# Seven half-size products for eight pairs of projected tiles

## The reference, cut to what matters

```python
h = rmsnorm(x, P['norm1_w'][l]) * (1 + sc1) + sh1
u_att, u_rw, u_ssd = split_cols(h @ P['w_in'][l], [ATT_COLS, RW_COLS, SSD_COLS])
```

## Time and profile before

| what | value |
|---|---|
| median of 3 runs | 1047.29 us (1043.87 to 1050.62) |
| the profiled execution | 1050.17 us |
| its span, first to last instruction | 1048.4 us |
| mean granted TensorE clock | 0.966 of full speed |
| TensorE busy | 929.7 us (89% of the span) |
| VectorE busy | 492.1 us (47%) |
| ScalarE busy | 286.3 us (27%) |

### The profile page before, as it was taken

One profiled execution on the slowest core, in us unless ns is written; L12 is line 12 of the kernel. 1 busy time (PEld: TensorE's weight loads), 2 busy tenths in 40 slices (PEclk: granted clock), 3 DMA queues, 4 the chain that ended last, 5 costly groups with the idle time before them and its releaser, 6 DMA issues. The chain is left out here.

```text
span 1048.4 us, 25535 instructions
## 1 busy us (share of the span) xinstructions
PE 929.7 (89%) x11081; PEld 663.2 (63%) x11081; DVE 492.1 (47%) x1349; ACT 286.3 (27%) x664; POOL 61.9 (6%) x91
## 2 busy tenths in 40 slices
PE   7899998777789999979989999887789999996796
PEld 4455566566668876646755566666677977664455
DVE  1362388657752443113546238966774252311135
ACT  3330317533211611110143031853321151111000
POOL 0000000000000030012000000000000003001120
PEclk9899999989999999999999999998899999998899
DMA  9869523421169979999852221342017968999993
GB/s 372 354 154 278 155 95 143 167 83 45 48 247 397 376 262 361 383 373 395 326 207 81 80 86 43 122 161 83 9 47 281 423 221 286 384 376 358 378 418 90
DMA packets 43735, 239.79 MB, mean 229 GB/s; under 512 B 5152, under 2 KB 8352, under 8 KB 20064
## 3 DMA queue, kind: packets, MB, share of 16 engines
q1 hardware_dynamic: 30192, 197.42, 48.9%
q0 software_dynamic: 9584, 34.35, 10.7%
q10 hardware_dynamic: 3840, 6.29, 1.9%
HBM read 211.29 MB, written 26.74 MB: 227 GB/s over the span
## 5 line engine op out<-in xcount | busy, mean ns | idle before, releaser
L1086 PE MATMUL bank<-sb_hT,sb_ring 128*128 128x385 f32 (+1 forms) x640 | 208.7, 496 | 4.4 <-ACT sb_hT L1825 4.4
L1086 PEld LDWEIGHTS bank<-sb_hT,sb_ring 128*128 128x128 f32 (+1 forms) x640 | 117.0, 189 | 91.2 <-issue 11.6
L1825 ACT ACTIVATE sb_u<-bank 128x256 f32<-128x256 f32 (+4 forms) x142 | 61.3, 463 | 237.6 <-PE bank L1086 225.7
L1086 PE MATMUL bank<-sb_arena 64*64 64x64 f32 (+5 forms) x1032 | 97.4, 334 | 11.0 <-DMA sb_arena<-weights 4.1
L1086 PEld LDWEIGHTS bank<-sb_arena 128*64 128x64 f32 (+2 forms) x1032 | 56.8, 145 | 36.7 <-issue 20.0
L2209 DVE SCALAR_TENSOR_TENSOR sb_xT<-bank,sb_mod,sb_xT 128x128 f32<-128x128 f32 x144 | 41.1, 346 | 69.8 <-PE bank L1086 69.6
L1086 PE MATMUL bank<-sb_ring,sb_arena 128*64 128x256 f32 (+3 forms) x544 | 64.5, 389 | 0.8
L1086 PE MATMUL bank<-sb_u,sb_arena 64*64 64x64 f32 (+2 forms) x744 | 58.9, 319 | 6.3 <-DMA sb_u<-weights 1.6
L1086 PE MATMUL bank<-sb_o,sb_ring 128*128 128x257 f32 (+1 forms) x384 | 64.3, 327 | 0.0
L1086 PEld LDWEIGHTS bank<-sb_o,sb_ring 128*128 128x128 f32 x384 | 58.0, 190 | 5.9
L1825 ACT ACTIVATE sb_tmp<-bank 128x128 f32<-128x128 f32 (+2 forms) x39 | 10.8, 277 | 185.1 <-PE bank L1086 185.0
(11 more groups left out here) (231 smaller groups left out, 1322.9 us busy)
## 6 DMA issues: line engine op xcount, KB each, us to landing
sb_ring<-weights SPq DMA_DIRECT2D x95, 1024.0 KB, 8.2
sb_arena<-weights SPq DMA_DIRECT2D x40, 1024.0 KB, 17.9
sb_u<-weights SPq DMA_DIRECT2D x22, 1024.0 KB, 11.6
sb_hT<-weights SPq DMA_DIRECT2D x10, 1024.0 KB, 17.3
sb_sq<-weights SPq DMA_DIRECT2D x8, 1024.0 KB, 16.1
x_slots<-sb_o POOLq DMA_DIRECT2D x1, 6912.0 KB, 39.5
sb_consts<-weights SPq DMA_DIRECT2D x6, 1024.0 KB, 19.7
sb_sq<-x_slots POOLq DMA_DIRECT2D x18, 256.0 KB, 7.9
```

Source lines behind the costliest of these rows:

```text
L1086: return nc.tensor.matmul(out, lhsT, rhs, start=start, stop=stop, skip_group_check=True)
L1825: return nc.scalar.activation(out, in_, func, **kw)
```

## The change

Eight of the ten pairs (1 to 7 and 9; not 0, and not 8, which holds the dt columns) are computed in another way. The weights of a pair are taken as a 2 x 2 of blocks, A11 and A12 for the first tile (the two halves of the depth), A21 and A22 for the second; h likewise as B11 and B21 (depth halves) of the first 193 columns and B12 and B22 of the last 192 (the sums use 193, one column overlapping). The four quarters of the result come from seven products of half the depth and half the columns (Winograd's form): A11 B11, A12 B21, S2 T2, S3 T3, S1 T1, S4 B22 and A22 T4, with four sums S of weight blocks for each pair and four sums T of h for each layer, and with six adds for each pair. All sums and adds are VectorE's. TensorE issues 28 matmuls of 193 or 192 columns for a pair in place of 16 of 385.

With it come:

- a new bank entry for each of six accumulations of a pair; the "corner" bank holds A11 B11 first, which ScalarE copies to `u` (`first_copied`), then A12 B21 is added in the bank, and ScalarE copies again when VectorE has used the first copy;
- the weight sums stand in ring places 3 and 4, so items of the projection use three places;
- VectorE's loop goes by pairs, its other work stands behind whole pairs in a new order, and qk_norm, key_factors and rotation come later;
- `AFTER_U` is moved by one tile for all but the low-rank products and dt_sums;
- two of the sums of h lie in `o`, so the zeros are written from a piece of 512 columns, in four transfers, once pair 1 is filled; the column of zeros of `o` is set again before the attention.

```diff
-AFTER_U = {2: ["lora0", "lora1"], 3: ["lora2", "lora3"], 4: ["key_squares"], 6: ["rw_values"], 8: ["bonus"],
-           12: ["qk_squares"], 13: ["v_columns"], 15: ["rotation"], 18: ["dt_sums"]}
+AFTER_U = {2: ["lora0", "lora1"], 3: ["lora2", "lora3"], 5: ["key_squares"], 7: ["rw_values"], 9: ["bonus"],
+           13: ["qk_squares"], 14: ["v_columns"], 16: ["rotation"], 18: ["dt_sums"]}
+PAIRED = [1, 2, 3, 4, 5, 6, 7, 9]
+PRODUCTS = [[("six", "v"), ("corner", "a")], [("seven", "v"), ("five", "v"), ("three", "v"), ("four", "v")]]
+HALF = 193
+LATE = W - HALF
+ITEM_SLOTS = 3
...
-            i = extra[0] if extra else min(range(len(HOMES) if wide else KEPT if lent else SLOTS), key=used)
+            i = extra[0] if extra else min(range(len(HOMES) if wide else KEPT if lent else
+                                                         ITEM_SLOTS if key[0] in ("u", "prod") else SLOTS), key=used)
...
-            filled(pool, "u", 0, 3)
-            pool.dma_start(x_slots.rearrange("(b p) c -> p b c", p=SLOT),
-                           bc(o_flat[0:SLOT, 0:D], 1, BLOCKS)).then_inc(slots_cleared, 16)
...
+            filled(pool, "prod", 0, 1, "four")
+            for j in range(2):
+                half = slice(j * (D // 2), (j + 1) * (D // 2))
+                pool.dma_start(x_slots[:, half].rearrange("(b p) c -> p b c", p=SLOT),
+                               bc(zeros, 1, BLOCKS)).then_inc(slots_cleared, 16)
+                pool.dma_start(y_slots[STORED * SLOT:, half].rearrange("(b p) c -> p b c", p=SLOT),
+                               bc(zeros, 1, BLOCKS - STORED)).then_inc(slots_cleared, 16)
...
+            def product(bank, left, right, start=True):
+                for k in range(4):
+                    last = mm(bank[:, 0:right.shape[2]], left[:, k * P:(k + 1) * P], right[:, k, :], start and k == 0, k == 3)
+                return last
+
+            def first_products(l, p, item):
...
+                corner = bank_ahead(pe, "prod", l, p, "corner")
+                product(corner, a11, hT[:, 0:4, 0:HALF]).then_inc(first_product, 1)
+                bank = open_bank(pe, "prod", l, p, "six")
+                pe.wait_ge(h_sums_ready, 4 * (l + 1))
+                pe.wait_ge(weight_sums_ready, 4 * n + 3)
+                product(bank, s2, t2).then_inc(psum_filled, 1)
+                bank = open_bank(pe, "prod", l, p, "corner")
+                pe.wait_ge(first_copied, n + 1)
+                product(bank, a12, hT[:, 4:8, 0:HALF], False).then_inc(psum_filled, 1)
+
+            def last_products(l, p, item):
...
+                product(open_bank(pe, "prod", l, p, "seven"), s3, t3).then_inc(psum_filled, 1)
+                product(open_bank(pe, "prod", l, p, "five"), s1, t1[:, :, 1:HALF]).then_inc(psum_filled, 1)
+                bank = open_bank(pe, "prod", l, p, "three")
+                pe.wait_ge(weight_sums_ready, 4 * n + 4)
+                product(bank, s4, hT[:, 4:8, HALF:W]).then_inc(psum_filled, 1)
+                product(open_bank(pe, "prod", l, p, "four"), a22, t4).then_inc(psum_filled, 1)
...
+            def corner(l, p):
+
+                out = u[:, U_ORDER[2 * p], 1:HALF + 1]
+                act.wait_ge(first_product, paired_before(l, p) + 1)
+                bank = banks[index["prod", l, p, "corner"] % 8]
+                f(out, bank[:, 0:HALF], ACT.Copy).then_inc(first_copied, 1)
+                bank = filled(act, "prod", l, p, "corner")
+                taken(act, "prod", l, p, "six")
+                f(out, bank[:, 0:HALF], ACT.Copy).then_inc(read("prod", l, p, "corner"), 1)
...
+            def h_halves(l):
...
+                dve.wait_ge(h_ready, KT * 3 * l + KT)
+                tt(t1, b12, b11, ALU.subtract).then_inc(h_sums_ready, 1)
+                tt(t3, b22, b12, ALU.subtract).then_inc(h_sums_ready, 1)
+                dve.wait_ge(h_sums_ready, 4 * l + 1)
+                tt(t2, b22, t1, ALU.subtract).then_inc(h_sums_ready, 1)
+                dve.wait_ge(h_sums_ready, 4 * l + 3)
+                tt(t4, t2, b21, ALU.subtract).then_inc(h_sums_ready, 1)
+
+            def weight_sums(l, p):
...
+                tt(s1, a21, a22, ALU.add).then_inc(weight_sums_ready, 1)
+                tt(s3, a11, a21, ALU.subtract).then_inc(weight_sums_ready, 1)
+                dve.wait_ge(weight_sums_ready, before + 1)
+                tt(s2, s1, a11, ALU.subtract).then_inc(weight_sums_ready, 1)
+                dve.wait_ge(weight_sums_ready, before + 3)
+                tt(s4, a12, s2, ALU.subtract).then_inc(weight_sums_ready, 1)
+
+            def quarters_of(l, p):
...
+                bank = filled(dve, "prod", l, p, "six")
+                dve.wait_ge(first_copied, paired_before(l, p) + 1)
+                tt(partial, bank[:, 0:HALF], upper[:, early], ALU.add).then_inc(read("prod", l, p, "six"), 1)
+                taken(dve, "prod", l, p, "six")
+                bank = filled(dve, "prod", l, p, "seven")
+                tt(lower[:, early], bank[:, 0:HALF], partial, ALU.add).then_inc(read("prod", l, p, "seven"), 1)
+                bank = filled(dve, "prod", l, p, "five")
+                tt(upper[:, late], bank[:, 0:LATE], partial[:, 1:HALF], ALU.add)
+                taken(dve, "prod", l, p, "seven")
+                tt(lower[:, late], bank[:, 0:LATE], lower[:, 2:HALF + 1], ALU.add).then_inc(read("prod", l, p, "five"), 1)
+                taken(dve, "prod", l, p, "five")
+                bank = filled(dve, "prod", l, p, "three")
+                tt(upper[:, late], bank[:, 0:LATE], upper[:, late], ALU.add).then_inc(read("prod", l, p, "three"), 1)
+                bank = filled(dve, "prod", l, p, "four")
+                tt(lower[:, early], lower[:, early], bank[:, 0:HALF], ALU.subtract).then_inc(read("prod", l, p, "four"), 1)
...
+                h_halves(l)
+                for p in range(U_TILES // 2):
...
+                    if p not in PAIRED:
+                        bank = filled(dve, "u", l, 2 * p)
+                        tile = U_ORDER[2 * p]
+                        v.tensor_copy(u[:, tile, 1:W + 1], bank[:, 0:W]).then_inc(read("u", l, 2 * p), 1)
+                    if p == 0:
                         token_shift(l, 6).then_inc(lora_in_ready, 1)
+                    if p + 1 in PAIRED:
+                        weight_sums(l, p + 1)
+                    if p == 3:
                         dve.wait_ge(kk_root_ready, l + 1)
                         link(tt(kdir, kdir, shaped(tmp[:, :], 2, W), ALU.mult))
+                    elif p == 5:
+                        bonuses(l)
+                    if p in PAIRED:
+                        quarters_of(l, p)
+                    if p == 1:
+                        key_squares(l)
+                    elif p == 2:
+                        token_shift(l, 4, 5).then_inc(rw_values_ready, 1)
+                    elif p == 3:
                         bonus_inputs(l)
+                    elif p == 4:
+                        decay_sums(l)
+                    elif p == 7:
                         qk_norm(l)
                         key_factors(l)
+                    elif p == 8:
                         rotation(l)
                         ssd_convolution(l, 0, 1)
+                    elif p == 9:
                         ssd_convolution(l, 2, 3).then_inc(conv_ready, 1)
+                v.memset(o[:, 0:4, P:LAT], 0.0)
                 attention(l)
```

More of the change, by code:

```diff
@@ L247, in psum_plan @@
         for c in range(U_TILES):
-            g("va"[c % 2], "u", l, c)
+            if c // 2 in PAIRED:
+                for name, consumer in PRODUCTS[c % 2]:
+                    g(consumer, "prod", l, c // 2, name)
+            else:
+                g("va"[c % 2], "u", l, c)
             for step in AFTER_U.get(c, ()):
@@ L422, in weight_stream @@
             out.append((("fixed", l, MOD_ITEMS + rest[0] // 2), ("u", l, rest[0] + 1)))
+        elif kind == "prod" and rest[1] == "six":
+            out.append((("fixed", l, MOD_ITEMS + rest[0]), ("prod", l, rest[0], "four")))
         elif kind == "out" and rest[0] % 2 == 0 and rest[1] == 0:
@@ L563, in program @@
         cols = sb("cols", 32)
-        AREN = 14390
+        AREN = 14442
         arena = sb("arena", AREN)
@@ L624, in program @@
         mixed_tiles = [x[:, i, :] for x in (mixed_r, mixed_k, mixed_v) for i in range(2)] + [mixed_lora[:, 0, :]]
+        at_o = [o_flat, 0, 4 * (W + 1)]
+        h_sums = [carve(rw, 4, HALF), carve(at_o, 4, HALF), carve(at_o, 4, HALF), carve(sums, 4, HALF)]
+        partial = carve(sums, HALF)
+        zeros = o_flat[0:SLOT, at_o[1]:at_o[1] + D // 2]
+        w_sums = [[ring[:, (ITEM_SLOTS + i) * ITEM + j * 4 * P:(ITEM_SLOTS + i) * ITEM + (j + 1) * 4 * P] for j in range(4)]
+                  for i in range(2)]
         lent = [ring, KEPT * ITEM, SLOTS * ITEM]
@@ L773, in read, with quarters, paired_before, projected @@
             return psum_read[consumer]
+        def quarters(item):
+            return [item[:, i * 4 * P:(i + 1) * 4 * P] for i in range(4)]
```

(19 more changed lines are left out.)

77 lines of the change are left out of this document (42 added, 35 removed).

## The result

The changed kernel takes 1059.56 us (median of 4 runs, 1058.61 to 1061.31), the kernel before 1045.87 us beside it. The ratio is 1.0131, 95% interval 1.0099 to 1.0164: slower by 13.7 us. The prediction was 1056.5 us, range 1044 to 1068; its +9.2 us would be a ratio of 1.0088, a little under that interval. The profiled execution took 1059.57 us with a span of 1057.8, 9.4 more than the span of before; that execution of before lay above its own median, the one of after on it, which is why the medians differ by more. Beside the other medians of before in this document (1045.8 to 1050.1 us) the changed kernel is 9.5 to 13.8 us slower.

A forecast was written before the change was run, and what follows sets the result against it. The prediction took VectorE's tail at the projection's end as the bound: 5.0 us late, less 0.9, plus 0.5 hand-overs, 4.6 us per layer. That is +9.2 us on 1047.29, median 1056.5, own range 1051 to 1063, whole range 1044 to 1068.

The forecast's parts named there:

- The end of the projection bounds, not TensorE's busy share: Projection: TensorE is full throughout, but VectorE has almost no room at the end, 3.8 us of slack behind the projections.
- TensorE's pair 10.37 to 9.2 us: Projection matmuls: 56 records of 164.6 ns replace 64 of 324 ns, giving back 1.17 us a pair.
- The third rival: Projection matmuls: weight loads of 189 ns bound the short matmuls, 7.8 us later per layer, median 1072.1; chance 9%.
- Pair 7 done at 126.7 us: Layer 0 projection: seven pairs gain 8.2 us less 3.7 us of stalls (1.5 and 2.2), against 131.21 us before.
- The tail of 31.2 us: VectorE's work from pair 7's end to the attention sums to 31.2 us, reaching it at 157.9 in place of 152.90.
- The wait of about 4 us for tile 16's bank costs nothing: TensorE behind pair 7 waits about 4 us, yet finishes pair 9 some 2 us before VectorE wants it.
- The wait of 0.89 us at 156.02 goes away: VectorE, start of attention: scores are then ahead, so 5.0 us late becomes 4.1 us.
- the mod weights' new place: Attention: second half of the first modulation chunk waits for pair 9's place, its MB taking 3.8 us, at no cost.
- The delay passes through the attention: Attention: VectorE is busy almost throughout and what follows waits for it, so 4.6 us per layer passes to the end.
- the first rival: Attention takes the delay back through VectorE's idles of 2.13 and 3.18 us: -0.7 us per layer, median 1045.9; chance 13%.
- 4.6 us per layer: Each layer's lateness into the attention: 4.1 us plus 0.5 for hand-overs, 9.2 us for both layers.
- The zeros in half rows: Zeros written in four transfers of half-length rows with the same bytes are done long before 158 us, costing nothing.

The follow-up runs named there:

- pair 9 plain: The changed kernel with only pair 9 back to sixteen full matmuls: 1051.21 us, ratio 1.0017 to the kernel before.
- the early tail: The changed kernel with qk_norm and key_factors ahead of pair 7's adds on VectorE: 1048.18 us, ratio 0.9979 to the kernel before.
- plain products: The changed kernel's new order, three ring places and halved rows of zeros, but no pair computed the new way: 1056.14 us, ratio 1.0091 to the kernel before.
- the mended version: The changed kernel with qk_norm and key_factors earlier, two stalls removed and the last two items' ring places exchanged: 1034.86 us, ratio 0.9859; repeated, 1036.55 us, 0.9886.
- The run with other places: The changed kernel with only the ring places of the last two pairs' items changed: 1059.05 us, ratio 1.0101 to the kernel before.
- no weight sums: The changed kernel without VectorE's four weight sums per pair, TensorE taking plain blocks instead: 1065.14 us, only the projection being read.

## Why the prediction was right, step by step

- *The end of the projection bounds, not TensorE's busy share.* Right, and shown from both sides: less work in the tail (pair 9 plain) and the same work elsewhere (the early tail) take back 1.1 and 1.5% of the time. The tail alone shrank by 3.9 and 7.3 us in them.
- *TensorE's pair 10.37 to 9.2 us.* Right (9.16, from the rows at 82.56 to 91.72 us of the changed kernel). The third rival, loads one after the other, fell by the spacing of 163.5 ns under loads of 199 ns. The Trainium skill, "TensorE: Matmul & The Clock Gate", section "Back-to-back issue gap", has two rules. The one for an isolated matmul, taken twice for a record, gives 2 x 82.9 = 166 ns at 193 columns, and the trace again agrees with it; it doesn't agree with the sustained one, by which the gain would have been 0.4 us a pair (an estimate from that page).
- *Pair 7 done at 126.7 us.* 129.30. The stalls were sized well: 1.06 for 1.5, 2.04 for 2.2, and one of 0.35 us at 64.84 us, where ScalarE comes from its sigmoids and a table load of 1.28 us, that I had not seen. Two terms were missing: 1.05 us by which this execution began later, and 1.7 us of slow matmuls behind the 2.04 us stall. The prediction had thought of a fall of the clock only at tile 16's bank, where it costs nothing; the same fall behind the stall of ScalarE's first copy lies on the path. Counted from the projection's start, pair 7 came 2.96 and 2.49 us earlier than before, in place of 4.5.
- *The tail of 31.2 us.* Right: 30.6, and the 0.5 us for hand-overs that I put on top of it was not needed. An add of 193 columns took 0.36 us (0.35), the sums of a pair 2.61 (2.7), the four over h 3.6 (3.7), hidden under the first tiles. Without the weight sums of pair 9 the tail would be only 0.5 us shorter, as TensorE is 2 us ahead there, the figure of the prediction.
- *The wait of about 4 us for tile 16's bank costs nothing.* Right in size (4.43) and in effect: it and the slow matmuls behind it fall where VectorE is last.
- *"The wait of 0.89 us at 156.02 goes away", and the mod weights' new place "costs nothing".* This step failed. I set 3.8 us for a MB and ended the count there, but the chunk's matmuls come ahead of the scores of the third maxima, and those came at the half clock. The 0.89 became 1.85 + 1.03. The price that I named for a VectorE that is on time, some 2 us on TensorE, was 2.7 to 2.9 us of waiting with plain products, and cost 3.3 and 5.6 us of the stretch there; in the mended version it was not more than 2.
- *The delay passes through the attention.* Too strict, in the other direction: the idles of 2.13 and 3.18 us shrank to 1.24 and 0.98, by 3.1 us, as the first rival had it. The two errors cancel: I forecast a gain of 0.9 us in the attention, and it measured 1.02 and 0.96. That this came out is luck. It is also at the edge of a sign that I had named for being wrong, an attention shorter by more than 1 us. The run with other places shows the two errors to be one thing: taking the DMA's wait away lets the 2.13 us return. VectorE has some 5 us of idle there in either version (6.2 before), and where it shows depends on what is late.
- *4.6 us per layer.* 4.94 and 5.54. The mis-sized term is TensorE's path to the end of pair 7 (1.5 and 2.0 us less gain than forecast), of which a tail that is 1.1 us shorter than forecast, with its hand-overs, takes back a part.
- *The zeros in half rows.* Right: VectorE enters the attention without waiting for them. From the first issue to the last landing the four transfers took 61.5 us (60.8 to 122.3), the two before 59.2 (61.3 to 120.5), with the same bytes and twice the rows. The Trainium skill, "DMA: Bandwidth & Descriptors", section "Specifications", gives 512 bytes as enough for the full rate, and the trace agrees: rows of 2 KB cost 4% more than rows of 4 KB, not twice as much.

So the forecast of +9.2 us holds against the spans (+9.4), and the median is 3.1 us above 1056.5, within its own range of 1051 to 1063. The agreement with the spans is closer than the mechanism was: the two stretches lost 10.5 us, and stages that the change doesn't touch gave 1 us back.

## What to carry to other kernels

An algorithm that moves work from the busiest engine to an idler one is decided where the idler one is not idle: draw up its timeline behind the last matmul group that everything hangs on, and count that, together with every stall that makes this group late. Here 67 us more on VectorE lost 1.3% in one order; moving two steps alone brought it level with the kernel before, and with two stalls and two ring places mended too it won 1.1 to 1.4%, with the same number of instructions. When a stage gives up buffers, look at which of its last items lies in a place that the next stage asks for first. And when a wait is removed in a stage with slack, look whether the idle turns up one step further on, as it did here in the changed kernel. Last, compare pieces of a trace that lie behind a common event, such as the end of pair 7: they repeated within 0.1 us, where whole executions differ by several.

## What the runs showed of the hardware

Short waits can cost more than their length. Windows of the changed kernel (length, busy PE, PEld, DVE, ACT, POOL; then PEclk, DMA share, GB/s): the first holds the stall of 2.04 us, the next two lie behind it and behind the 4.43 us one; 0.64 and 0.57 mean that part of the stretch ran at 1.2 of 2.4 GHz.

```profile
116.00:119.00 3.00, 2.65 (x17) 2.35 (x15) 0.00 (x0) 2.90 (x8) 0.00 (x0) 1.00 1.00 240
120.60:125.40 4.80, 4.71 (x20) 4.65 (x21) 0.36 (x1) 0.82 (x2) 0.00 (x0) 0.64 0.30 121
142.60:149.70 7.10, 7.03 (x24) 6.85 (x24) 6.72 (x15) 0.33 (x1) 0.00 (x0) 0.57 0.01 2
```

The same stall of 2.04 us in the run with other places was followed by full speed:

```profile
119.80:124.00 4.20, 4.18 (x27) 4.18 (x28) 0.70 (x2) 0.82 (x2) 0.00 (x0) 1.00 0.80 330
```

From the stall's end to the next product but one are 4.70 us in the changed kernel and 3.02 here, 1.7 us less. That is part of the 2.7 by which this projection stretch was shorter in layer 0. The other 1.0 lies in the first 40 matmul records of the projection, behind TensorE's wait of 2.18 us for h: they took 14.47 and 13.43 us, and in other traces from 12.15 to 14.86. The edit itself reaches neither place.

Five versions have this same stall in both layers, ten cases in all. In five of them the clock in the 4 us behind it was 0.59 to 0.63 (the changed kernel in both layers, the early tail in layer 0, pair 9 plain and no weight sums in layer 1), in the other five 1.00; a slow case cost 1.7 us each time. The stalls of 1.06 and 0.35 us were never followed by slow matmuls in these traces, those of 4.4 us each time. What decides at 2 us stays open. A wait of that length is thus worth removing even where it looks small, and one execution's total can differ by a few microseconds from another's for this alone.
